# A hybrid streaming encoder step: wide products that nobody reads, ahead of the sample tile's state reads and between their heads

## The reference

```
def step(s, inp):                      # gated delta rule, one block of tokens
    ...
    v_new = u - jnp.einsum('bhcd,bhde->bhce', wk, s)
    o = (jnp.einsum('bhcd,bhde->bhce', qc * jnp.exp(gcum)[..., None], s)
         + jnp.einsum('bhij,bhje->bhie', jnp.einsum('bhid,bhjd->bhij', qc, kc) * decay, v_new))

def step(s, inp):                      # GLA
    ...
    o_inter = jnp.einsum('bhcd,bhde->bhce', qc * jnp.exp(b), s)
```

## Time and profile before

| | before |
|---|---|
| median of 3 runs | 3581.76 us (3579.33 to 3584.27) |
| the profiled execution: its own time | 3591.44 us |
| span in its trace | 3589.7 us, 62851 instructions |
| PE busy | 3338.9 us, 93% of the span |
| DVE, ACT, POOL busy | 1315.5, 721.9 and 1031.2 us |
| mean granted TensorE clock | 0.943 |

### The profile page before, as it was taken

The page is one execution under the profiler, slowest core; times in us unless marked ns, Lnnn a source line. Parts: engine busy times, 40 slices in busy tenths (PEclk is TensorE's granted clock), DMA queues, the critical chain, the costliest instruction groups (busy, mean ns, idle before and its releaser), DMA issues. The chain is left out here.

```text
span 3589.7 us, 62851 instructions
## 1 busy us (share of the span) xinstructions
PE 3338.9 (93%) x26790; PEld 3128.5 (87%) x26790; DVE 1315.5 (37%) x1704; ACT 721.9 (20%) x1254; POOL 1031.2 (29%) x675
## 2 busy tenths in 40 slices
PE   7989988888599999999998999899989999999997
PEld 7978777777499999999998997566689999999997
DVE  6630034555453333333333110255533333333333
ACT  3212122233232000000002001366612100001004
POOL 3443033443113222322224341011033222322223
PEclk8989967888699999999999999899999999999999
DMA  5222111110321111111110233466421111111101
GB/s 194 77 91 71 59 52 33 51 43 29 125 96 53 54 46 35 35 41 53 47 35 24 94 106 114 143 171 174 113 59 42 53 42 40 35 41 53 41 29 53
DMA packets 271471, 246.42 MB, mean 69 GB/s; under 512 B 23689, under 2 KB 236258, under 8 KB 271289
## 3 DMA queue, kind: packets, MB, share of 16 engines
q1 hardware_dynamic: 264152, 217.43, 19.2%
q0 software_dynamic: 7136, 26.35, 2.4%
HBM read 191.70 MB, written 54.13 MB: 68 GB/s over the span
## 5 line engine op out<-in xcount | busy, mean ns | idle before, releaser
L326 PE MATMUL PS<-hT_high,w_split_tiles 128*128 128x384 f32 x5904 | 1203.4, 336 | 18.2 <-POOL w_split_tiles L340 11.0
L326 PEld LDWEIGHTS PS<-hT_high,w_split_tiles 128*128 128x128 f32 x5904 | 1042.9, 189 | 18.8 <-POOL w_split_tiles L340 11.2
L326 PE MATMUL PS<-hT_low,w_split_tiles 128*128 128x384 f32 x2952 | 674.2, 336 | 0.0
L326 PE MATMUL PS<-ffn_act_split,w_down_split 128*128 128x384 f32 x3024 | 530.0, 335 | 4.9 <-issue 4.9
L326 PEld LDWEIGHTS PS<-ffn_act_split,w_down_split 128*128 128x128 f32 x3024 | 526.8, 188 | 5.2 <-issue 5.2
L326 PEld LDWEIGHTS PS<-hT_low,w_split_tiles 128*128 128x128 f32 x2952 | 529.6, 189 | 0.0
L731 DVE TENSOR_TENSOR xT<-xT,PS 128x1152 f32<-128x1152 f32 x168 | 227.5, 1354 | 300.8 <-PE PS L326 300.8
L507 POOL CAST w_split_tiles<-w_raw_tiles 128x1024 fp32r<-128x1024 f32 x44 | 46.9, 1067 | 434.2 <-PE PS L326 322.1
L507 POOL CAST w_split_tiles<-attention_oT 128x1024 fp32r<-128x1024 f32 x42 | 43.7, 1041 | 341.2 <-PE PS L326 332.4
L668 ACT CAST ffn_act_split<-attention_oT 128x1152 fp32r<-128x1152 f32 x22 | 25.5, 1159 | 483.5 <-PE PS L326 348.1
L668 ACT CAST ffn_act_split<-ffn_room 128x1152 fp32r<-128x1152 f32 x22 | 25.5, 1160 | 483.5 <-PE PS L326 348.0
(11 more groups left out here) (430 smaller groups left out, 4802.0 us busy)
## 6 DMA issues: line engine op xcount, KB each, us to landing
w_raw_tiles<-in_ffn_w_gu_dram SPq DMA_DIRECT2D x44, 512.0 KB, 3.9
attention_oT<-in_ffn_w_gu_dram SPq DMA_DIRECT2D x44, 512.0 KB, 3.9
cache_k<-in_cache_c_k_dram SPq DMA_DIRECT2D x64, 256.0 KB, 5.1
cache_v<-in_cache_c_v_dram SPq DMA_DIRECT2D x64, 256.0 KB, 5.0
ffn_room<-in_ffn_w_down_dram SPq DMA_DIRECT2D x11, 1024.0 KB
attention_oT<-in_ffn_w_down_dram SPq DMA_DIRECT2D x11, 1024.0 KB
rest_dram<-w_raw_tiles SPq DMA_DIRECT2D x36, 256.0 KB, 2.1
w_raw_tiles<-in_c_w_qkv_dram POOLq DMA_DIRECT2D x18, 512.0 KB, 4.7
```

What stands on the lines that cost most here:

```text
L326: m = nc.tensor.matmul(PS[:, banks + j, 0:GN], wl if p == 2 else wh, sl if p == 1 else sh, start=(n == 0 and p == 0), stop=(n == last and ...
```

## The change

In `sample_reads`, and nowhere else, PE gets 24 more products. `keep_warm` multiplies 128 x 128 weights from `spr` with 512 columns of `spr` and writes PSUM bank 1, where nobody reads the result. Eight of them stand ahead of the reads, and one stands behind each of the 16 delta head groups (the one behind the eighth head of a bank comes after the semaphore that releases ACT's copy). PE also waits for `pt_ready` of tile 1, so that bank 1 is free. The three groups of reads and everything behind them are as they were; no other engine's work changes.

```
             def sample_reads(k):
+                def keep_warm():
+                    mm(PS[:, 1, :], spr[:, 0:P], spr[:, 0:512], start=True, stop=True)
                 pe.wait_ge(states_in, 16 * 6)
                 free_quad(k)
                 wt_ready.wait(pe, k)
+                pt_ready.wait(pe, k + 1)
+                for _ in range(8):
+                    keep_warm()
                 for bank, src, done in ((6, wt[:], 1), (7, qt[:, k % 3], 1)):
                     for h in range(H):
                         r, m = dn_rows(h)
                         for b in range(BS):
                             t = slice(LS * b, LS * b + LS)
                             x = mm(PS[r, bank, m * P + LS * b:m * P + LS * b + LS], Ss[r, m, b], src[r, m, t], start=True, stop=True)
+                        if h < H - 1:
+                            keep_warm()
                     x.then_inc(read_mm, 1)
+                    keep_warm()
```

## The result

The change makes the kernel slower: ratio 1.0061 to the kernel before, 95% interval 1.0048 to 1.0074. The median is 3606.63 us (6 runs, 3603.52 to 3610.7); the kernel before gave 3585.57 us over 6 runs (3579.33 to 3589.79), 3.8 us more than over the first three. So +21.1 us, where +17.1 was forecast, and the median lies 0.6 us above the top of the stated range.

The account below looks back on a forecast made before the run. PE alone bounds the sample reads, its clock halving without a pause. Eight ahead 1.91, 4.2 heads 5.6, 11.8 heads 27.5, GLA reads 11.0: 46.0 us against 28.9, +17.1, so 3581.76 becomes 3598.9 us, range 3586 to 3606.

Parts of the forecast that it names:

- PE alone is on the path, and the loss reaches the end in full: Sample reads, 28.9 us: only PE works and a barrier ends the stage, so all +17.1 us reaches the kernel's end.
- A seam lets nothing overlap: Between head and wide product, the array part changes without overlap; head plus product 1.33 us full clock, 2.33 lower.
- The rival without a seam: Sample reads: head with wide product 0.953 us, 1.76 at lower clock; +7.3 us, or 3571.6 us (chance 0.04) if clock holds.
- The clock falls among the heads, after about four: Delta reads: full clock lasts 5.6 us after the eight, 4.2 heads; the other 11.8 run at the lower clock.
- the wide product's size at a seam: Wide product behind a head: 0.389 us less 0.07 is 0.32 at full clock, 0.628 less 0.07 is 0.56 at lower.
- The base: Whole kernel: median of 3581.76 us before the change, to which +17.1 was added; runs spread 2.5 us either side.
- The upper bound: Sample reads: clock falls once the eight are through, all 16 heads cost 2.33 us; 50.2 us, +21.3, 3603.

Follow-up runs that it names:

- e2: Changed kernel without the eight wide products ahead, the sixteen between heads kept: 3604.42 us against 3588.15 for the kernel before, ratio 1.0049.
- e4: Changed kernel without the eight ahead, each product between heads now 64x64 weights by 128 columns in the head's corner: 3595.08 against 3588.15 us, ratio 1.0024.
- e7: Changed kernel without the eight ahead, one wide product behind every second head only: 3606.99 us against 3587.2 for the kernel before, ratio 1.0053.
- e1: Changed kernel without the sixteen products between heads, the eight ahead kept: 3594.99 us against 3588.15 for the kernel before, ratio 1.0019.
- e8: Changed kernel with four wide products behind each head, one behind each bank's last head: 3627.33 us against 3587.2 for the kernel before, single run.
- e9: Changed kernel without the eight ahead, products between heads cut to 16 moving and 64 weight columns: 3598.61 against 3590.85 us, single run each.
- e6: Kernel before with reads issued in turn over heads in different array parts, plus the eight wide products ahead: 3575.8 against 3587.2 us, ratio 0.9973.
- e5: Kernel before with reads issued in turn over heads in different array parts, no wide products: 3579.15 against 3587.2 us, ratio 0.9975.
- e3: Changed kernel without the eight ahead, products between heads cut to 16 moving columns, still 128 weight columns: 3607.04 against 3588.15 us, ratio 1.0057.

## Why the prediction was right or wrong, point by point

- **PE alone is on the path, and the loss reaches the end in full**: right. Stretch +20.5, medians +21.1, DVE's wait +20.5, the stretches behind unchanged in this pair of traces. That median and stretch agree to 0.6 us is closer than the spread of the runs warrants.
- **A seam lets nothing overlap**: right. With sixteen products in the same places the stretch grows by 19.5 us over the whole array (e2) and by 3.7 in the head's corner (e4), and by half with half the seams (e7). The rival without a seam (a head and its wide product at 0.95 and 1.76 us) was out from the first row of the trace after. The rule of the Trainium skill that a change of tiling mode drains the engine ("TensorEngine Tiling (Array Packing)", Key Properties) agrees with this, and its price here is about 0.79 us of 2.12 a head at the lower clock.
- **The clock falls among the heads, after about four**: right. 5.8 us behind the eight (5.6 said), four heads (4.2 said). But e1 gave 2.4 us, so the closeness was in part luck; the forecast should have taken it as a range. With the heads one after the other the clock held in no run through half the delta reads, not with four wide products a head either (e8). The rule of the Trainium skill that a busy engine gets and keeps the full clock ("TensorE: Matmul & The Clock Gate", Why this matters for your kernels) doesn't hold here: 41.6 us of unbroken work at 0.50 in the trace after.
- **The step that failed: the wide product's size at a seam**, "wide 0.628 - 0.07 = 0.56" and "0.389, less 0.07 is 0.32". It was read from L2834, where wide products follow each other and the load of the next weights lies under the one before. Behind a change of the array's part it doesn't: the record is 0.50 and 0.79 us, and it costs 511.87 to 512.30 = 0.43 and 518.51 to 519.24 = 0.73. Its load starts with it, where L2834's starts 0.23 us ahead (the rows behind e9). e9 shows that the record becomes shorter by what the load does. The kernel before had a row with the right neighbours, L1715 at 464.73, and it gives the 0.79. Twelve heads at 0.17 and four at 0.11 are 2.5 us of the missing 3.4; a head alone at the lower clock was 1.81 and not 1.77 (0.5 us), the eight 2.02 and not 1.91, and 12 of 16 heads ran at the lower clock, not 11.8.
- **The base**: the other reason that the median left the range; neither alone would have taken it out. The sum stood on 3581.76 us, three runs; six gave 3585.57, and 22 more gave 3588.15. With the measured growth of the stretch, +20.5, the forecast would have been 3602.3, in range but still 4 us low for the base alone; with the right base and the predicted +17.1 it would have been 3602.7. The spread that I took, 2.5 us, was that of three runs.
- **The upper bound** (all heads at the lower clock, +21.3) was worked out with the same too small seam; with 2.54 us a head it is 2.0 + 40.6 + 11.0 - 28.9 = +24.7.

What stays open is why the clock falls 2.4 us after the eight in one execution and 5.8 in the three others with them (the change, e6, e8). The traces show one regularity. Counted from the end of the last product of `exponents` (509.59 before, 507.77 in e1, 507.66 in the changed kernel), the clock fell 5.5 to 5.6 us later in the kernel before, in e1 and in every run without the eight, whatever stood between the heads, and 8.9 to 9.0 us later in those three. Each trace is one execution, so how often the eight bring the longer time is not known.

## What to carry to other kernels

Before work is put between small products to keep an engine's clock up, see whether neighbours overlap: here a product of 16 columns over the whole array cost as much as two thirds of the 512-column one, because the heads on either side no longer overlapped (0.48 of its 0.79 us) and the weight load lay bare in the rest. What small products in separate parts of the array need is their order: in turn over the parts, they took 13.8 us where they had taken 28.9, with the clock falling as early. And price an added operation from a row with the same neighbours, not only of the same shape.

## What the runs showed of the hardware

- Records in different corners of the array run abreast: at the full clock the records of the first group start 0.029 us apart in turn (128 in 3.91 us, e5) and 0.045 head by head (80 in 3.63 us); 128 GLA records over four parts took 3.61 us against 11.03, both at the lower clock.
- A product can run beside the next head's reads if they use the other corner: its two records cover 0.67 us (522.53 to 522.78 + 0.42) and made a head's period only 0.19 us longer at the lower clock (e4).
- Where the part of the array in use changes, the weight load starts with its product and not ahead of it: 0.29 of 0.31 us at the lower clock (e3), and with half the weight columns both became 0.11 us shorter (e9).
- Busy is not enough for the full clock: 59.5 us without a pause at 0.50 (e8).
